# Spare rounded matrix products between the blocks of an up projection

## The reference

```
def conv_ffn(h, w_up, conv_w, conv_b, w_down):
    gate, val = jnp.split(h @ w_up, 2, axis=-1)
    gp = jnp.pad(gate, ((0, 0), (CONV_WIDTH - 1, 0), (0, 0)))
    conv = conv_b + sum over kk of gp[:, kk:kk + S] * conv_w[kk]
    return (jax.nn.gelu(conv, approximate=True) * val) @ w_down
```

## Time and profile before

| | us |
|---|---|
| median of three runs | 1030.02 |
| the profiled execution, its own time | 1034.57 |
| its span, first to last instruction | 1032.7 |
| TensorE busy | 987.7 |
| VectorE busy | 556.7 |
| ScalarE busy | 402.7 |
| up projection, products of `three` | 124.37 |
| down projection, its share of the chain of waits | 54.96 |

### The profile page before, as it was taken

One profiled execution on the slowest core, in us unless ns is written; L12 is line 12 of the kernel. 1 busy time (PEld: TensorE's weight loads), 2 busy tenths in 40 slices (PEclk: granted clock), 3 DMA queues, 4 the chain that ended last, 5 costly groups with the idle time before them and its releaser, 6 DMA issues.

```text
span 1032.7 us, 15441 instructions
## 1 busy us (share of the span) xinstructions
PE 987.7 (96%) x5874; PEld 675.7 (65%) x5874; DVE 556.7 (54%) x1209; ACT 402.7 (39%) x793; POOL 107.5 (10%) x141
## 2 busy tenths in 40 slices
PE   7999999999999999899999999989999999999984
PEld 7977899999886889777633434338677734334332
DVE  5765656666446754775423433457675513434364
ACT  5465456555435545683312112123474312121110
POOL 0721001111001100151001000000132001000000
PEclk9999999999999999999999999999999999999997
DMA  9872576645545453808999999996357999999992
GB/s 328 205 250 88 190 244 205 203 164 177 191 164 198 143 173 105 324 3 357 397 423 421 410 421 420 421 396 234 115 243 302 394 418 421 411 421 420 422 406 94
DMA packets 96110, 292.31 MB, mean 283 GB/s; under 512 B 11086, under 2 KB 48126, under 8 KB 72478
## 3 DMA queue, kind: packets, MB, share of 16 engines
q1 hardware_dynamic: 96030, 291.24, 74.1%
HBM read 289.98 MB, written 1.25 MB: 282 GB/s over the span
## 4 chain that ended last, share of the span: by engine, by line
PE 79%; DVE 8%; DMA 6%; ACT 3%; issue 2%; POOL 1%; SPq 0%; DVEq 0%; POOLq 0%; ACTq 0%
PE ps L1035 36%; PE ps L1488 16%; PE ps L1526 9%; DMA arena<-in_moe_w_up 3%; DMA w<-in_moe_w_up 3%; DVE yTr L2383 2%; PE ps L1141 2%; PE ps L1171 2%; PE ps L1152 2%; PE ps L977 2%; PE ps L1463 1%; PE ps L1536 1%; PE ps L1336 1%; DVE plo L1748 1%; PE ps L984 1%
## 5 line engine op out<-in xcount | busy, mean ns | idle before, releaser
L1748 DVE TENSOR_TENSOR plo<-w,phi 128x1024 fp32r<-128x1024 f32 (+3 forms) x147 | 177.4, 1226 | 135.0 <-ACT phi L2564 134.9
L2564 ACT CAST phi<-w 128x1024 fp32r<-128x1024 f32 (+3 forms) x147 | 148.5, 1032 | 139.0 <-PE ps L1035 131.8
L2383 DVE SCALAR_TENSOR_TENSOR yTr<-ps,small,yTr 32x512 fp32r<-32x512 f32 x112 | 83.7, 748 | 181.0 <-ACT yTr L2861 179.4
L1488 PE MATMUL ps<-w,arena 128*64 128x512 f32 x464 | 135.6, 594 | 1.3 <-DMA w<-in_moe_w_up 1.3
L1035 PE MATMUL ps<-hTr,phi 128*128 128x256 f32 x472 | 133.1, 282 | 0.0
L1035 PE MATMUL ps<-hTr,plo 128*128 128x256 f32 x472 | 132.5, 281 | 0.0
L1035 PE MATMUL ps<-yTr,phi 128*128 128x256 f32 x472 | 132.5, 281 | 0.0
L1035 PE MATMUL ps<-phi,hTr 128*128 128x512 f32 (+2 forms) x240 | 93.9, 391 | 0.8 <-issue 0.7
L1035 PE MATMUL ps<-phi,yTr 128*128 128x512 f32 (+2 forms) x240 | 93.5, 389 | 0.7 <-DVE hTr L1740 0.7
L1035 PEld LDWEIGHTS ps<-yTr,phi 128*128 128x128 f32 x472 | 90.2, 191 | 0.0
L1035 PEld LDWEIGHTS ps<-hTr,phi 128*128 128x128 f32 x472 | 88.8, 188 | 0.2
(11 more groups left out here) (362 smaller groups left out, 1732.8 us busy)
## 6 DMA issues: line engine op xcount, KB each, us to landing
w<-in_moe_w_down SPq DMA_DIRECT2D x31, 1024.0 KB, 18.8
w<-in_moe_w_up SPq DMA_DIRECT2D x31, 1024.0 KB, 18.2
w<-in_moe_w_gate SPq DMA_DIRECT2D x27, 1024.0 KB, 15.8
w<-in_w_up SPq DMA_DIRECT2D x22, 1024.0 KB, 7.6
arena<-in_moe_w_up SPq DMA_DIRECT2D x19, 1024.0 KB, 16.2
arena<-in_moe_w_gate SPq DMA_DIRECT2D x15, 1024.0 KB, 20.8
arena<-in_moe_w_down SPq DMA_DIRECT2D x13, 1024.0 KB, 21.0
w<-in_w_out SPq DMA_DIRECT2D x6, 2048.0 KB, 10.2
```

The lines of the kernel that those rows point to most:

```text
L1488: ins_ = e.matmul(bank[64 * ee:64 * ee + 64, :], xg[:, k, o:o + 64], half_view(i, kind, p, ee, ab)[:, c, :], start=(k == 0), stop=(k == 7))
L1748: e.tensor_tensor(plo[:, 0:m], slots[u % 3][:, j * m:j * m + m], phi[:, 0:m].bitcast(F32), ALU.subtract).then_inc(s_cut)
L2383: ins_ = e.scalar_tensor_tensor(y_parts[t][other, part], psum[2 + hf][own_, :], slot_gate[own_, p:p + 1], y_parts[t][own_, part].bitcast(F ...
L2564: e.copy(pieces[p % 4][0][:, 0:m], slots[u % 3][:, j * m:j * m + m]).then_inc(s_cast)
```

## The change

A table gives for eight of the eleven blocks a list of widths. Ahead of the block's 96 products TensorE issues one fp32r product for each width in the list: stationary `hTr[:, 0, 0:128]`, moving the first `width` columns of the 512 that slices 1 and 2 of `hTr` make, into PSUM bank 4, each as an accumulation group of its own. Nothing reads what they write. They are twelve products: five of 416 columns, three of 512, three of 128 and one of 64, which is 4064 columns. Blocks 0, 2 and 7 get none.

```diff
@@ -81,6 +81,7 @@
 NEAR = 4
+WIDTHS = {1: (416,), 3: (512,), 4: (128,), 5: (416, 416, 416), 6: (64,), 8: (416,), 9: (512, 512), 10: (128, 128)}
 NHALF = 23
@@ -1257,6 +1258,9 @@
             await_empty("h2a", "h2b")
             for u in range(NJ // 2):
+                for width in WIDTHS.get(u, ()):
+                    e.matmul(psum[4][:, 0:width], hTr[:, 0, 0:128], hTr[:, 1:3, :].rearrange("p c t -> p (c t)")[:, 0:width],
+                             start=True, stop=True)
                 feat3("up", 2 * u, h1, 512, lambda c, h: h * 256 + c * 128, first_piece(f"up{u}"))
```

## The result

Nine runs of the changed kernel gave a median of 1032.69 us (1032.14 to 1034.51), nine of the kernel before beside them 1030.02 (1029.70 to 1031.07): ratio 1.0022, 95% interval [1.0012, 1.0032]. The forecast was 1028.8, with a range up to 1032.3. The profiled execution took 1034.51 us, its span is 1032.6; before, these were 1034.57 and 1032.7.

What follows compares the result with a forecast made beforehand. TensorE alone was taken to bound the up projection. Products 2.06 plus edges 0.2 minus 8 x 0.43 for faster blocks gave -1.2 us, so 1030.02 - 1.2 = 1028.8 us, range 1027.7 to 1032.3.

Steps and rivals of the forecast that it cites:

- What bounds the stage: Up projection: TensorE alone sets its 124.37 us; VectorE and ScalarE wait for it, not the other way.
- The twelve products and their edges: Spares ahead of the blocks: 2.06 us for the products, all on TensorE's path, plus 0.2 us for edges.
- Rival D: Up projection: each spare group breaks the pipeline at both edges, 0.09 to 0.18 us each; 1033.5 to 1035.0 us; chance 0.06.
- The pace behind them: Blocks 1 to 10: eight of ten go from 117.8 to 113.3 ns a product, 0.43 us less each.
- What follows: Behind the up projection: everything shifts with the stage's end, counted in full; 1030.02 - 1.2 = 1028.8 us.
- rival C: Up projection: the pace stays, none or one block fast; +1.8 to +2.3, 1031.8 to 1032.3 us; chance 0.17.
- rival B: Up projection: two to six blocks fast, spares may slow a fast block; +1.4 to -0.3, 1029.7 to 1031.4 us; chance 0.30.
- The shift reaching the end: Down projection and experts: the stage's change passes to the end in full, since expert loads wait for TensorE and shift too.

Runs made afterwards that it cites:

- lower group: Runs of the unchanged kernel between 1029.1 and 1032.7 us, 29 of 45 on one chip; its profiled execution with the stage at the fast step took 1030.55 us.
- upper group: Runs of the unchanged kernel between 1034.2 and 1035.6 us, 16 of 45 on one chip; the profiled execution with the stage at the slow step lies there.
- second session: A later set of timed runs of the unchanged kernel beside changed ones; 10 of its 33 runs of the unchanged kernel were over 1033 us.

## Why the prediction was wrong

*What bounds the stage* was right: TensorE alone, without a wait in it, at both paces.

*The twelve products and their edges* were right: 2.06 + 0.2 predicted. Measured against the fast stage, 122.33 - 119.70 = 2.63, less 0.43 for the slow block 4, is 2.20 in all. The spares' own pieces in the chain sum to 1.91, the rest is edges. Narrow ones do cost what the row of L1381 said: in the changed kernel the 128 takes 0.06 us itself and makes the next step 0.17 instead of 0.11, 0.12 together. Rival D, breaks of the pipeline at 0.09 to 0.18 an edge, is out: the edges of all eight groups sum to about 0.3. (A slip that changes nothing: 4064 / 2.4 + 12 x 2.5 is 1723, not 1724.)

*The pace behind them* was right in size, 0.43 us a block, and nearly in count, nine of ten against the eight I took. That the count came out was luck: I counted 14 stretches as draws, as an outcome of how the starts fall. It isn't a draw. Over all traces a single 128 turned the pace 16 times of 16 (the pair of them ahead of block 10 left it fast three times, as two turns would); 416, 512 and 64 left the fast step each time, from either pace, though 512 and 64 stood behind a slow block only once each; 256 behind a slow block changed nothing. That the spares' outcome could have been read from the trace of before I can't show: only the 416 stood there.

*What follows* is the step that failed, and in one clause: "I set it against the median of the runs, 1030.02, since the two differ by 4.55 us everywhere in the same way as far as I can see." They differ in this one stage. The profiled execution of before had it at 117.8 ns, 124.37 us; the nine runs beside the changed kernel were by their times all in the lower group, and the profiled execution of that group has it at 113.3, 119.70 us. None of the nine was itself profiled, so their pace is concluded from the group. The 4.67 between the two stages makes up the 4.55. So the sum's last term, 8 x 0.43 us to be won, was zero against those runs, and its other two terms plus block 4 remain: 2.06 + 0.2 + 0.43 = +2.7 us. Measured: +2.67. The prediction had this as a side remark in rival C, with the right product (1056 x 4.44 ns = 4.7), and gave it too little: "nothing else in the trace speaks for that" was true, but the times beside the trace did. An execution that is 4.55 us longer than three runs that agree within 1.1 us is a finding to be explained before its rows are used as the kernel's own. The range, too, ended at the price without a block thrown back into the slow step, 0.4 under the result; rival B had such a block, but not together with a stage that is fast already.

*The shift reaching the end* was right on the whole. In the pair of profiles it doesn't look so: the changed kernel's stage is 2.04 us shorter and its span only 0.1. Part of that is the start, 0.7 later; the rest was lost among the experts, where the long DMA wait took 27.59 us in the chain instead of the 26.48 of the earlier trace rows:

```profile
659.99 27.59 DMA w<-in_moe_w_up
```

One pair can't tell that from scatter: over the twelve traces what lies behind the stage took 778.6 to 780.9 us, and the profile of the changed kernel has the largest of these; it is also the longest of its nine runs, 1.8 over their median. Between the two profiles of the unchanged kernel the gain of the stage reached the end in full, and 24 spares behind the stage cost their whole price.

So the change does fix a fault, but one that the runs it was measured against didn't have. Where before's runs are mostly slow, its ratio would be under 1: against the upper group of the second session (median 1034.8) its 1032.69 is 2.1 us less. That is worked out across sessions, not measured side by side. The version that is never measured behind either is the single 416 ahead of block 1: 0.9969 [0.9953, 0.9985] where before enters slow in most runs, 0.9999 [0.9990, 1.0008], so no gain and no loss, where it doesn't, and 2.9 us better than the change on one chip.

## What to carry to other kernels

Before a trace is used for a sum, hold the profiled execution's own time against the runs: if it lies off by much more than they scatter, look for the stage that may have run in another mode, and profile the same kernel twice. When equal instructions run at two steady paces in one trace, ask first which of them the timed runs have. And where one product sets a mode for all that follow, as the 416 did here, one is enough; each further one is pure price.

## What the runs showed of the hardware

A stream of fp32r products with 256 moving columns and a new 128 x 128 stationary operand each holds one of two paces, 113.3 or 117.8 ns, at a granted clock of 1.00 in both. It kept either for as long as 1056 products, through changes of bank and of weight piece. A single product of another width in the stream decided the pace of what followed: 64, 416 and 512 columns left 113.3, 128 turned one pace into the other (16 of 16), 256 left the slow one as it was (2 of 2). Most streams of 512 columns ran at 229 ns, the down projection in all twelve traces; but they have a second pace too: the layer at 51 us, 48 products, ran at 233.4 ns in four of the traces (in the second profile of the unchanged kernel its starts go from 51.11 to 62.08 us) and at 229.4 to 229.6 in the other eight. Which pace the up projection enters differs from execution to execution of the same program, and the shares differ by session. Not every stream varies so: the 96 products of 256 columns at 39 us had 117.8 ns in all twelve traces, `xq2` behind its 416 columns 113.3 in all. Why there are two paces, the runs don't show.
